# Two transformer blocks on one core: the last feed-forward's operands move to the arena and are made behind each residual

## The chip, the cores and the metric

The kernel runs on one core of a Trainium2 chip. The metric is the device time of one execution in microseconds (us). Times in the text are us from the start of the profiled span unless they are durations.

TensorE multiplies matrices, VectorE and ScalarE work elementwise, GpSimd helps with a few additions, and SyncE issues nearly all DMAs. Each engine runs its own list of instructions in order, and semaphores tie the lists together.

## What is computed

The input is one sequence of 512 tokens with 1024 features. Two blocks run one after the other. The first has a feed-forward, a mixer (a short convolution beside a gated delta rule) and another feed-forward. The second has two layers: gated linear attention with memory attention and a convolutional feed-forward, then sparse attention ("nsa") with memory attention and a convolutional feed-forward. The change touches the end of the last layer, which is in the reference:

```python
        h = h + jnp.concatenate([main.astype(xn.dtype), mo.astype(xn.dtype)], axis=-1) @ w_out[i]
        h = h + conv_ffn(rmsnorm_2(h, norm_ffn[i]), w_up[i], conv_w[i], conv_b[i], w_down[i])

def conv_ffn(x, w_up, conv_w, conv_b, w_down):
    S = x.shape[1]
    u = x @ w_up
    u_pad = jnp.pad(u, ((0, 0), (CONV_WIDTH - 1, 0), (0, 0)))
    hc = conv_b
    for j in range(CONV_WIDTH):
        hc = hc + conv_w[j] * u_pad[:, j:j + S]
    a, b = split_cols(hc, (FFN_DIM, FFN_DIM))
    return (jax.nn.silu(a) * b) @ w_down
```

FFN_DIM is 2816, so w_up has 5632 columns.

## The kernel before

The residual stream h is kept transposed in SBUF as `hT`: 128 features on the partitions, 8 blocks of features k, 512 tokens. A dense stage is a list of weight panels and output tiles. A panel of 128 output columns is 128 x 1024 fp32 values; it is loaded by SyncE into one of four slots of `raw`. Each fp32 product is made of three matmuls on two halves of either operand: the high half rounded to the type float32r, and the rest. For weights, ScalarE writes the high half wH (line 407, `split_hi`) and VectorE the low half wL = raw - wH (line 445, `split_lo`); there are two places for them, so a panel's halves can be written when TensorE has finished with the panel two before. For the activations, ScalarE writes `x_hi` = hT x gain into xH (line 826) and VectorE `x_lo` = hT x gain - xH into xL (line 831).

A tile of a features stage is 128 output features by 512 tokens in one PSUM bank. It takes 8 steps k, each of three matmuls with 512 columns: lines 570 (wH with xH), 571 (wH with xL) and 572 (wL with xH). The weights are loaded as the stationary operand and x streams past as the moving one.

The stages around the change, in order:

- The attention ends with `upper_act` (line 2763) and `rest_dve` (line 2710), which write the last pieces of xH and xL.
- `nsa_out` multiplies by w_out: 8 tiles, written as a loop of two iterations with 4 panels and banks 0 to 3. VectorE adds each finished tile to hT (line 808, called the residual below; its count is `h_from("nsa_out")`).
- `refill_act` then makes the operands of the last feed-forward on ScalarE: four squares for the norm, a wait for all matmuls of nsa_out (since they read xH), eight x_hi, the split of the next stage's panel 1 (`split_second`), four more squares. On VectorE the eight x_lo follow the last residual.
- `ffn3_up`: 11 iterations of 4 tiles, 44 tiles in all. In its first tile TensorE waits for `x_ready` step by step, so it starts when x_lo(0) is there ("GRADUAL"). GpSimd adds up the squares (line 878) and, after tile 2, TensorE sums them over the partitions (line 883); ScalarE makes `rstd` of that (lines 846, 848), and only then VectorE can evacuate tile 0 (line 2300).
- `ffn3_down`: unrolled, 22 steps over 8 banks, lines 757 to 759, with the moving operands g_hi and g_lo. Then the last norm and the output.

`gla_out`, the output stage of the layer before, has code of its own (`gla_out_pe`, lines 737 to 739): step f multiplies into all 8 banks one after the other. Its operand is m_hi, m_lo for the steps 0 and 1 and xH, xL for the steps 2 to 7.

xH, xL, wH, wL and hT are allocated one by one. The rest of SBUF is the arena: 14 regions of 2048 fp32 values per partition, of which other tensors are views at fixed offsets:

```python
        R = 2048
        at_arena = (nc.sbuf_usable_end - 4 * 14 * R) // 32 * 32
        g_hi = nc.alloc_sbuf_tensor_at("g_hi", [P, 4, S], F32R, offset=at_arena + 4 * 12 * R)
        g_lo = nc.alloc_sbuf_tensor_at("g_lo", [P, 4, S], F32R, offset=at_arena + 4 * 13 * R)
        m_hi = nc.alloc_sbuf_tensor_at("m_hi", [P, 2, S], F32R, offset=at_arena + 4 * (7 * R + R // 2))
        m_lo = nc.alloc_sbuf_tensor_at("m_lo", [P, 2, S], F32R, offset=at_arena + 4 * 7 * R)
```

In the last feed-forward, the regions 0 to 5 hold g, 6 and 8 the tiles of the convolution, 12 and 13 g_hi and g_lo. The regions 7, 9, 10 and 11 are free while ffn3_up runs.

## Time and profile before

| | us |
|---|---|
| median of 3 runs | 2510.38 (2506.29 to 2510.39) |
| the profiled execution | 2514.45 |
| its span | 2512.6 |
| TensorE busy | 2429.6 (97%) |
| VectorE busy | 1339.6 (53%) |
| ScalarE busy | 960.4 (38%) |
| GpSimd busy | 152.2 (6%) |
| nsa_out, first matmul | 2082.45 |
| ffn3_up, first matmul | 2130.22 |
| ffn3_down, first matmul | 2372.57 |

The span is the time between the first and the last record of the profiled execution; the device time around it is 1.85 us longer. TensorE's spans are modelled: each matmul is given a length that overlaps the next one's start, so the pace is read from the distance between starts, never from the lengths. A few matmul records can be missing, so a distance is taken from the first and last start and the number of steps that the program has between them.

### The profile page before, as it was taken

The page shows a single profiled execution, that of the slowest core. Times are in us where ns is not written, and L with a number is a line of the kernel's source. Part 1 is how long each engine was busy: PE and PEld are TensorE (multiplying, and loading weights), DVE is VectorE, ACT ScalarE, POOL GpSimd, SP SyncE. Part 2 cuts the span into 40 slices and gives each one's busy share as a digit, 9 for nine tenths or more (in the row PEclk, how much of TensorE's full clock was granted, in tenths as well). Part 3 has the DMA queues.
Part 4 walks back from the last instruction along what each step waited for, and adds up shares of the span by engine and source line. Part 5 has one row for each costly group of instructions (what it writes and reads, how often), then busy time and mean ns, then how long its engine had stood idle before and what let it go on. Part 6 is the DMA issues. An engine that isn't in the chain of part 4 may idle for free.

```text
span 2512.6 us, 32091 instructions
## 1 busy us (share of the span) xinstructions
PE 2429.6 (97%) x12218; PEld 1973.2 (79%) x12218; DVE 1339.6 (53%) x2054; ACT 960.4 (38%) x1461; POOL 152.2 (6%) x130
## 2 busy tenths in 40 slices
PE   7999999998999999999899999999999888999999
PEld 6888886678878888877887788878877557888887
DVE  4434337665454334345775766643535873666633
ACT  4222226632343223245334533432324773433423
POOL 3000001013010000021000100000110000000001
PEclk9999999999999999999999999999999999999999
DMA  4333222220123332223122233222843102333322
GB/s 138 92 100 93 100 85 76 76 67 10 51 76 92 100 96 88 99 85 78 47 63 76 84 98 94 92 95 90 171 140 101 45 16 67 93 100 92 101 92 76
DMA packets 319121, 215.80 MB, mean 86 GB/s; under 512 B 49289, under 2 KB 302748, under 8 KB 319016
## 3 DMA queue, kind: packets, MB, share of 16 engines
q1 hardware_dynamic: 315752, 200.40, 27.3%
q0 software_dynamic: 3264, 13.94, 1.6%
q8 instruction: 72, 1.18, 0.2%
q14 instruction: 33, 0.27, 0.0%
HBM read 212.17 MB, written 8.44 MB: 88 GB/s over the span
## 4 chain that ended last, share of the span: by engine, by line
PE 84%; DVE 8%; ACT 5%; issue 2%; DMA 1%; POOL 0%; POOLq 0%; ACTq 0%; DVEq 0%
PE bank L570 16%; PE bank L572 16%; PE bank L571 16%; PE bank L759 6%; PE bank L757 6%; PE bank L758 6%; PE bank L932 1%; DVE wL L445 1%; ACT wH L407 1%; DVE arena L2651 1%; PE bank L2138 1%; PE bank L1620 1%; PE bank L1634 1%; PE bank L2560 1%; DVE arena L2690 1%
## 5 line engine op out<-in xcount | busy, mean ns | idle before, releaser
L570 PE MATMUL bank<-xH,wH 128*128 128x512 f32 x1928 | 769.1, 399 | 14.8 <-DVE wL L445 6.4
L572 PE MATMUL bank<-xH,wL 128*128 128x512 f32 x1928 | 756.6, 392 | 0.0
L571 PE MATMUL bank<-xL,wH 128*128 128x512 f32 x1928 | 756.4, 392 | 0.0
L445 DVE TENSOR_TENSOR wL<-raw,wH 128x1024 fp32r<-128x1024 f32 (+1 forms) x357 | 448.6, 1257 | 523.6 <-ACT wH L407 522.9
L407 ACT ACTIVATE wH<-raw 128x1024 fp32r<-128x1024 f32 (+1 forms) x357 | 374.6, 1049 | 752.4 <-PE bank L572 337.5
L570 PEld LDWEIGHTS bank<-xH,wH 128*128 128x128 f32 x1928 | 363.8, 189 | 105.9 <-issue 27.1
L571 PEld LDWEIGHTS bank<-xL,wH 128*128 128x128 f32 x1928 | 363.9, 189 | 80.7 <-issue 5.3
L572 PEld LDWEIGHTS bank<-xH,wL 128*128 128x128 f32 x1928 | 363.6, 189 | 79.3 <-issue 1.2
L757 PE MATMUL bank<-g_hi,wH 128*128 128x512 f32 x704 | 277.9, 395 | 1.2 <-DVE wL L445 1.2
L759 PE MATMUL bank<-g_hi,wL 128*128 128x512 f32 x704 | 278.9, 396 | 0.0
L758 PE MATMUL bank<-g_lo,wH 128*128 128x512 f32 x704 | 278.0, 395 | 0.0
L2268 ACT ACTIVATE arena<-arena,par 128x512 f32<-128x512 f32 x88 | 63.5, 724 | 270.1 <-DVE arena L2300 270.1
L757 PEld LDWEIGHTS bank<-g_hi,wH 128*128 128x128 f32 x704 | 132.2, 188 | 34.3 <-DVE wL L445 2.5
L758 PEld LDWEIGHTS bank<-g_lo,wH 128*128 128x128 f32 x704 | 132.2, 188 | 32.5
L759 PEld LDWEIGHTS bank<-g_hi,wL 128*128 128x128 f32 x704 | 132.2, 188 | 31.7
L2300 DVE TENSOR_TENSOR arena<-bank,rstd 128x512 f32<-128x512 f32 x88 | 60.6, 691 | 86.7 <-PE bank L572 81.0
L784 ACT ACTIVATE arena<-arena 128x512 f32<-128x512 f32 x44 | 27.6, 631 | 173.8 <-DVE arena L791 173.8
L878 POOL TENSOR_TENSOR rstd<-sq 128x512 f32<-128x512 f32 x7 | 10.2, 1453 | 1289.3 <-ACT sq L841 1289.3
L793 DVE TENSOR_TENSOR arena<-bank,rstd 128x512 f32 (+1 forms) x44 | 30.2, 691 | 103.2 <-PE bank L572 103.2
L932 PEld LDWEIGHTS bank<-ident,arena 128*128 128x128 f32 (+3 forms) x402 | 46.4, 146 | 49.0 <-issue 34.4
L932 PE MATMUL bank<-ident,arena 128*128 128x128 f32 (+3 forms) x402 | 61.2, 293 | 23.2 <-DMA arena<-in_x 9.3
L791 DVE TENSOR_TENSOR arena<-bank,rstd 128x512 f32<-128x512 f32 x44 | 30.2, 691 | 85.6 <-PE bank L572 80.2
(351 smaller groups left out, 2739.2 us busy)
## 6 DMA issues: line engine op xcount, KB each, us to landing
raw<-in_ffn_w_in SPq DMA_DIRECT2D x88, 512.0 KB, 3.7
raw<-in_w_up SPq DMA_DIRECT2D x88, 512.0 KB, 3.7
raw<-in_ffn_w_out SPq DMA_DIRECT2D x44, 512.0 KB, 3.4
raw<-in_w_down SPq DMA_DIRECT2D x44, 512.0 KB, 3.5
raw<-in_w_mix_in SPq DMA_DIRECT2D x28, 512.0 KB, 3.7
raw<-in_w_kv_shared SPq DMA_DIRECT2D x12, 512.0 KB, 9.0
rel_wide<-rel_rows POOLq DMA_DIRECT2D x12, 512.0 KB, 11.0
arena<-rel_wide POOLq DMA_DIRECT2D x12, 448.0 KB, 4.1
```

The lines of the kernel that those rows point to most:

```text
L407: nc.scalar.activation(hi[:, 0:n], raw[:, k, 0:n], ACT.Copy).then_inc(sem("w_hi"), 1)
L445: nc.vector.tensor_tensor(lo[:, 0:n], raw[:, k, 0:n], hi[:, 0:n].bitcast(F32), ALU.subtract)\
L570: pe.matmul(o, wh, xa, start=a, stop=False)
L571: pe.matmul(o, wh, xb, start=False, stop=False)
L572: last = pe.matmul(o, wl, xa, start=False, stop=z)
L757: pe.matmul(bank[m][:], wh, gh, start=f == 0, stop=False)
L758: pe.matmul(bank[m][:], wh, gl, start=False, stop=False)
L759: last = pe.matmul(bank[m][:], wl, gh, start=False, stop=f == NF - 1)
L791: nc.vector.tensor_tensor(sg[:, t, :], bank[t][:], rstd[:], ALU.mult).then_inc(sem("evac_dve"), 1)
L932: return pe.transpose(o, i, ident[0:k, 0:k])
L2268: nc.scalar.activation(cv[:, t, :], us[:, t, :], ACT.Copy, scale=conv_columns(s, i, t)[2])\
L2300: nc.vector.tensor_tensor(us[:, t, :], bank[t][:], rstd[:], ALU.mult).then_inc(sem("evac_dve"), 1)
```

## The change

1. The operands of ffn3_up get tensors of their own, x2_hi (regions 9 and 10 of the arena) and x2_lo (two halves, regions 11 and 7), in place of xH and xL. `filled` and `operand` pick the tensor.
2. x_hi(k) and square(k) follow residual(k) on ScalarE within nsa_out, behind the split of the panel after the next; x_lo(k) follows residual(k+1) on VectorE. Only those of block 7 are behind the last residual. The wait for all matmuls of nsa_out is gone.
3. nsa_out has one iteration of 8 panels and 8 tiles in banks 0 to 3, 0 to 3, and is so unrolled. The same change in `out_stage` has no other user.

On ScalarE, at the end of the attention, through nsa_out (L477 is the loop) and to the norm of ffn3_up; before:

```order
L477 UNCONDITIONAL_BRANCH
L407 ACTIVATE wH<-raw 128x1024 x4
L477 REGISTER_ALU
L477 COMPARE_AND_BRANCH
L407 ACTIVATE wH<-raw 128x1024 x4
L841 ACTIVATE sq<-hT 128x512 x4
L826 ACTIVATE xH<-hT,par 128x512 x8
L407 ACTIVATE wH<-raw 128x1024
L841 ACTIVATE sq<-hT 128x512 x4
L407 ACTIVATE wH<-raw 128x1024 x3
```

and now, from the last panels of nsa_out on (line 415 is the split, 838 x_hi, 854 the square):

```order
L415 ACTIVATE wH<-raw 128x1024
L838 ACTIVATE x_hi<-hT,par 128x512
L854 ACTIVATE sq<-hT 128x512
L838 ACTIVATE x_hi<-hT,par 128x512
L415 ACTIVATE wH<-raw 128x1024
L854 ACTIVATE sq<-hT 128x512
L415 ACTIVATE wH<-raw 128x1024 x3
```

The eight x_hi and the squares, which stood together, stand now one by one behind a split each; the second x_hi in the excerpt is block 7's, ahead of the split of ffn3_up's panel 1.

On VectorE at the same place, the last two tiles of nsa_out and what follows; before:

```order
L445 TENSOR_TENSOR wL<-raw,wH 128x1024
L808 SCALAR_TENSOR_TENSOR hT<-bank,hT 128x512
L445 TENSOR_TENSOR wL<-raw,wH 128x1024
L808 SCALAR_TENSOR_TENSOR hT<-bank,hT 128x512
L831 SCALAR_TENSOR_TENSOR xL<-hT,par,xH 128x512 x8
L445 TENSOR_TENSOR wL<-raw,wH 128x1024 x4
```

and now (line 453 is the split, 816 the residual, 844 x_lo; x_lo_58 is the second half of x2_lo):

```order
L453 TENSOR_TENSOR wL<-raw,wH 128x1024
L816 SCALAR_TENSOR_TENSOR hT<-bank,hT 128x512
L844 SCALAR_TENSOR_TENSOR x_lo_58<-hT,par,x_hi 128x512
L453 TENSOR_TENSOR wL<-raw,wH 128x1024
L816 SCALAR_TENSOR_TENSOR hT<-bank,hT 128x512
L844 SCALAR_TENSOR_TENSOR x_lo_58<-hT,par,x_hi 128x512 x2
L453 TENSOR_TENSOR wL<-raw,wH 128x1024 x4
```

Six of the eight x_lo have moved ahead of the last residual.

On TensorE at the border from nsa_out (L345 ends its loop) to ffn3_up; before:

```order
L572 MATMUL bank<-xH,wL 128x512
L345 REGISTER_ALU
L345 COMPARE_AND_BRANCH
L570 MATMUL bank<-xH,wH 128x512 [waits x_ready,w_lo,evac_dve]
L571 MATMUL bank<-xL,wH 128x512
L572 MATMUL bank<-xH,wL 128x512
L570 MATMUL bank<-xH,wH 128x512 [waits x_ready]
```

and now (lines 578 to 580 are the three matmuls; x_hi is x2_hi, x_lo_57 the first half of x2_lo):

```order
L580 MATMUL bank<-xH,wL 128x512
L578 MATMUL bank<-x_hi,wH 128x512 [waits x_ready,w_lo,evac_dve]
L579 MATMUL bank<-x_lo_57,wH 128x512
L580 MATMUL bank<-x_hi,wL 128x512
L578 MATMUL bank<-x_hi,wH 128x512 [waits x_ready]
```

The loop's instructions are gone and the moving operands are the new tensors, here and in all of ffn3_up. The diff:

```diff
@@ -177,6 +177,14 @@
         m_lo = nc.alloc_sbuf_tensor_at("m_lo", [P, 2, S], F32R, offset=at_arena + 4 * 7 * R)
         m_hi_f = m_hi[:].bitcast(F32)
 
+        x2_hi = nc.alloc_sbuf_tensor_at("x2_hi", [P, KD, S], F32R, offset=at_arena + 4 * 9 * R)
+        x2_lo = [nc.alloc_sbuf_tensor_at(f"x2_lo{u}", [P, 4, S], F32R, offset=at_arena + 4 * r * R)
+                 for u, r in enumerate((11, 7))]
+
+        def operand(x, k):
+
+            return x[k // 4][:, k % 4, :] if isinstance(x, list) else x[:, k, :]
+
         def region(a, n=1):
             return arena[:, a * R:(a + n) * R]
 
@@ -203,10 +211,10 @@
             return {"bank": b, "rows": width, "cols": S, "token": False, "by": by,
                     "terms": [(j, nk, q * cols + at, width, x0 + q) for q in range(k)]}
 
-        def up_stage(k, w, f):
+        def up_stage(k, w, f, xs=(xH, xL)):
 
             return Dense(f"ffn{k}_up", NF // 2, [[panel(w, KD, c + P * u, P, 2 * P)] for c in (0, FF) for u in range(2)],
-                         [features(b, b, P, 0) for b in range(4)], (xH, xL), xfill(f))
+                         [features(b, b, P, 0) for b in range(4)], xs, xfill(f))
 
         def down_stage(k, w):
 
@@ -215,8 +223,8 @@
                       "terms": [(f, P, m * P, P, f) for f in range(NF)]} for m in range(KD)]
             return Dense(f"ffn{k}_down", 1, panels, tiles, (g_hi, g_lo), None, by_rows=True)
 
-        def ffn(k, w_in, w_out, f):
-            return [up_stage(k, w_in, f), down_stage(k, w_out)]
+        def ffn(k, w_in, w_out, f, xs=(xH, xL)):
+            return [up_stage(k, w_in, f, xs), down_stage(k, w_out)]
 
         def tokens(b, j, cols, t, by="dve"):
 
@@ -239,8 +247,8 @@
 
         def out_stage(name, w, f):
 
-            return Dense(name, 2, [[panel(w, KD, P * j, P, 4 * P)] for j in range(4)],
-                         [features(b, b, P, 0) for b in range(4)], (xH, xL), xfill(f))
+            return Dense(name, 1, [[panel(w, KD, P * j, P)] for j in range(KD)],
+                         [features(b % 4, b, P, 0) for b in range(KD)], (xH, xL), xfill(f))
 
         mem_sq = region(11).rearrange("p (k m) -> p k m", m=M)
 
@@ -325,7 +333,7 @@
                   [features((1, 0)[t % 2], t, P, 0) for t in range(6)],
                   (xH, xL), xfill(8)),
             out_stage("nsa_out", A["w_out_2"][1], 9)]
-        stages += ffn(3, A["w_up_2"][1], A["w_down_2"][1], 10)
+        stages += ffn(3, A["w_up_2"][1], A["w_down_2"][1], 10, (x2_hi, x2_lo))
         plan = Plan(stages)
         nc_block = ctx.enter_context(nc.Block())
 
@@ -560,13 +568,13 @@
                         wh, wl = hi[0:nrow, first:first + width], lo[0:nrow, first:first + width]
                         if tile["token"]:
                             o = acc[0:tile["rows"], tile["at"]:tile["at"] + width]
-                            xa, xb = xh[0:nrow, x, tile["x"]], xl[0:nrow, x, tile["x"]]
+                            xa, xb = operand(xh, x)[0:nrow, tile["x"]], operand(xl, x)[0:nrow, tile["x"]]
                             pe.matmul(o, xa, wh, start=a, stop=False)
                             pe.matmul(o, xa, wl, start=False, stop=False)
                             last = pe.matmul(o, xb, wh, start=False, stop=z)
                         else:
                             o = acc[0:width, 0:tile["cols"]]
-                            xa, xb = xh[0:nrow, x, 0:tile["cols"]], xl[0:nrow, x, 0:tile["cols"]]
+                            xa, xb = operand(xh, x)[0:nrow, 0:tile["cols"]], operand(xl, x)[0:nrow, 0:tile["cols"]]
                             pe.matmul(o, wh, xa, start=a, stop=False)
                             pe.matmul(o, wh, xb, start=False, stop=False)
                             last = pe.matmul(o, wl, xa, start=False, stop=z)
@@ -820,15 +828,20 @@
             name, at = GAINS[f]
             return column(name, at + k)
 
+        def filled(f, k):
+
+            return (x2_hi[:, k, :], operand(x2_lo, k)) if f == 10 else (xH[:, k, :], xL[:, k, :])
+
         def x_hi(act, f, k, ready):
 
             act.wait_ge(*ready)
-            nc.scalar.activation(xH[:, k, :], hT[:, k, :], ACT.Copy, scale=gain(f, k)).then_inc(sem("x_hi"), 1)
+            nc.scalar.activation(filled(f, k)[0], hT[:, k, :], ACT.Copy, scale=gain(f, k)).then_inc(sem("x_hi"), 1)
 
         def x_lo(dve, f, k):
 
+            hi, lo = filled(f, k)
             dve.wait_ge(sem("x_hi"), xbase(f) + k + 1)
-            nc.vector.scalar_tensor_tensor(out=xL[:, k, :], in0=hT[:, k, :], scalar=gain(f, k), in1=xHf[:, k, :],
+            nc.vector.scalar_tensor_tensor(out=lo, in0=hT[:, k, :], scalar=gain(f, k), in1=hi.bitcast(F32),
                                            op0=ALU.mult, op1=ALU.subtract).then_inc(sem("x_ready"), 1)
 
         def square(act, r, k, ready, scale=1.0):
@@ -3013,8 +3026,15 @@
             act.wait_ge(*matmuls_done("nsa_q"))
             mem_out_act(act, 1, xH[:, 6:8, :])
             attend_act(act)
-            dense_act(act, "nsa_out", nothing)
-            refill_act(act, 10, 7, "nsa_out", "ffn3_up")
+            residual_done = h_from("nsa_out")
+
+            def block_act(k):
+                x_hi(act, 10, k, residual_done(k))
+                square(act, 7, k, residual_done(k))
+            dense_act(act, "nsa_out", nothing, extra={(0, k + 1): lambda k=k: block_act(k) for k in range(KD - 1)})
+            x_hi(act, 10, KD - 1, residual_done(KD - 1))
+            split_second(act, "ffn3_up")
+            square(act, 7, KD - 1, residual_done(KD - 1))
             conv_up_act(act, "ffn3_up", conv_evac_act, lambda: g_first_act(act, 3), hook=lambda: rstd_act(act, 7))
             down_act(act, 3)
             last_squares_act(act)
@@ -3104,9 +3124,9 @@
             dense_dve(dve, "nsa_q", evac_scaled(aq_place, rstd[:]),
                       extra={(0, r): lambda r=r: mem_round_dve(dve, 1, r) for r in range(NROUND)})
             attend_dve(dve)
-            dense_dve(dve, "nsa_out", residual(1.0))
-            for k in range(KD):
-                x_lo(dve, 10, k)
+            dense_dve(dve, "nsa_out", residual(1.0),
+                      extra={(0, k + 1): lambda k=k: x_lo(dve, 10, k) for k in range(KD - 1)})
+            x_lo(dve, 10, KD - 1)
             conv_up_dve(dve, "ffn3_up", conv_evac_dve, lambda: g_first_dve(dve, 3), hook=lambda: norm_dve(dve, 7))
             conv_end_dve(dve, "ffn3_up")
             down_dve(dve, 3, 1.0, None)
```

## Rows read from the trace of the kernel before

**Rows 1.** The page's head: span; engine, busy time, share, instructions.

```profile
span 2512.6 us, 32091 instructions
PE 2429.6 (97%) x12218; PEld 1973.2 (79%) x12218; DVE 1339.6 (53%) x2054; ACT 960.4 (38%) x1461; POOL 152.2 (6%) x130
```

**Rows 2.** Timeline of TensorE, nsa_out's end: start, duration, instruction, [idle before, releaser].

```profile
2127.50 0.39 PE L572 MATMUL bank<-xH,wL 128*128 128x512 f32 x1
2130.22 0.47 PE L570 MATMUL bank<-xH,wH 128*128 128x512 f32 x1 [2.33 <-DVE xL L831]
2130.53 0.44 PE L571 MATMUL bank<-xL,wH 128*128 128x512 f32 x1
...
2131.19 0.63 PE L570 MATMUL bank<-xH,wH 128*128 128x512 f32 x1
...
2134.17 0.39 PE L571 MATMUL bank<-xL,wH 128*128 128x512 f32 x1
```

**Rows 3.** Stretches: length, engines' busy time (instructions), TensorE's granted clock, DMA share, GB/s.

```profile
2130.90:2134.10 3.20, 3.20 (x9) 2.51 (x8) 3.20 (x6) 3.20 (x6) 0.00 (x0) 0.50 0.00 0
...
2160.00:2360.00 200.00, 199.90 (x882) 165.21 (x881) 136.88 (x171) 76.47 (x98) 0.00 (x0) 1.00 0.32 96
```

**Rows 4.** Timeline of ScalarE, nsa_out's end and ffn3_up's start.

```profile
2122.55 1.06 ACT L407 ACTIVATE wH<-raw 128x1024 fp32r<-128x1024 f32 x1 [4.38 <-PE bank L572]
...
2127.93 5.01 ACT L826 ACTIVATE xH<-hT,par 128x512 fp32r<-128x512 f32 x8 [0.66 <-PE bank L572]
```

**Rows 5.** Timeline of VectorE, the same stretch.

```profile
2127.93 0.69 DVE L808 SCALAR_TENSOR_TENSOR hT<-bank,hT 128x512 f32<-128x512 f32 x1 [3.06 <-PE bank L572]
2128.68 6.03 DVE L831 SCALAR_TENSOR_TENSOR xL<-hT,par,xH 128x512 fp32r<-128x512 f32 x8
2134.63 1.21 DVE L445 TENSOR_TENSOR wL<-raw,wH 128x1024 fp32r<-128x1024 f32 x1
2140.13 2.24 DVE L445 TENSOR_TENSOR wL<-raw,wH 128x1024 fp32r<-128x1024 f32 x1 [4.29 <-ACT wH L407]
```

**Rows 6.** Instructions by line, 2085 to 2136: ns min/median/max, first and last start.

```profile
L831 DVE SCALAR_TENSOR_TENSOR xL<-hT,par,xH x8: 737/737/1389, 2128.7 to 2134.0; 128x512 fp32r<-128x512 f32 x8
L826 ACT ACTIVATE xH<-hT,par x8: 706/706/722, 2127.9 to 2132.2; 128x512 fp32r<-128x512 f32 x8
L841 ACT ACTIVATE sq<-hT x4: 613/616/633, 2123.5 to 2126.7; 128x512 f32<-128x512 f32 x4
```

**Rows 7.** Timeline of GpSimd, all of it from 2060 to 2190.

```profile
2124.74 1.28 POOL L878 TENSOR_TENSOR rstd<-sq 128x512 f32<-128x512 f32 x1 [101.65 <-ACT sq L841]
2126.82 2.70 POOL L878 TENSOR_TENSOR rstd<-rstd,sq 128x512 f32<-128x512 f32 x2 [0.81 <-ACT sq L841]
2134.49 6.80 POOL L878 TENSOR_TENSOR rstd<-rstd,sq 128x512 f32<-128x512 f32 x4 [4.96 <-ACT sq L841]
```

**Rows 8.** One matmul line of gla_out (L738), of ffn3_down (L758), of nsa_out (L571).

```profile
L738 PE MATMUL bank<-xL,wH x48: 388/389/398, 1354.2 to 1386.2; 128*128 128x512 f32 x48
...
L738 PE MATMUL bank<-m_lo,wH x16: 394/394/394, 1343.0 to 1353.5; 128*128 128x512 f32 x16
...
L758 PE MATMUL bank<-g_lo,wH x167: 398/399/400, 2380.0 to 2496.2; 128*128 128x512 f32 x167
...
L571 PE MATMUL bank<-xL,wH x60: 389/389/395, 2087.1 to 2127.3; 128*128 128x512 f32 x60
```

**Rows 9.** Timelines of VectorE and TensorE, the attention's end and nsa_out's start.

```profile
2080.71 1.41 DVE L2710 TENSOR_TENSOR xL<-bank,xH 64x512 fp32r<-64x512 f32 x2 [7.01 <-ACT xH L2763]
...
2082.45 0.49 PE L570 MATMUL bank<-xH,wH 128*128 128x512 f32 x1 [2.42 <-DVE xL L2710]
```

**Rows 10.** Timelines of TensorE and VectorE, the norm and first evacuation of ffn3_up.

```profile
2148.23 1.03 PE L883 MATMUL bank<-rstd,ones 128*128 128x512 f32 x2
...
2153.53 1.29 DVE L2300 TENSOR_TENSOR arena<-bank,rstd 128x512 f32<-128x512 f32 x2 [2.72 <-ACT rstd L848]
...
2154.57 0.39 PE L570 MATMUL bank<-xH,wH 128*128 128x512 f32 x1
```

## The prediction

> **What bounds the kernel now.** I read the engines' busy shares first: TensorE is busy 97% of 2512.6 us [rows 1], so a change counts if it moves TensorE's idle time or the pace of its matmuls, and nothing else does. Next I read TensorE's instructions in order of time where nsa_out ends and ffn3_up begins, and looked for a break in the spacing of starts. The last matmul of nsa_out starts at 2127.50, the first of ffn3_up at 2130.22, after 2.33 us of idle that ends with VectorE's L831 [rows 2]. From 2131.19 to the eleventh matmul at 2134.17, starts are 2.98 / 7 = 0.43 us apart, against 0.227 elsewhere [rows 2, 8], and in that stretch the granted clock is 0.50, so 1.2 GHz in place of the 2.4 GHz of the steady part of ffn3_up, which shows 1.00 [rows 3]. The engine had idled for 2.33 us just before.
>
> Why it idles: ScalarE may write xH only when nsa_out's last matmul has read it, so x_hi starts at 2127.93 and needs 0.706 us for one [rows 4, 6]. VectorE's first x_lo starts at 2128.68 and takes 1389 ns in place of the usual 737, while GpSimd has two adds running from 2126.82 for 2.70 us [rows 6, 7]; 2128.68 + 1.39 = 2130.07, and the matmul starts 0.15 later.
>
> The third view is the one that this change turns on: one line's instructions, sorted by the tile that they read, with count and first and last start. In gla_out, the same three lines of code run with moving operands m_hi, m_lo for 16 steps of three matmuls and xH, xL for 48 steps. With m_lo: (1353.5 - 1343.0) / 15 = 0.700 us a step; with xL: (1386.2 - 1354.2) / 47 = 0.681 [rows 8]. ffn3_down, whose moving operands are g_hi and g_lo, gives (2496.2 - 2380.0) / 166 = 0.700; nsa_out, with xH and xL, (2127.3 - 2087.1) / 59 = 0.681 [rows 8]. So a matmul starts every 0.2333 us or every 0.2267. The weights lie in wH and wL in all four. gla_out changes its bank after every step with either operand, so the bank does not set the pace. What the slow ones share is that m_hi, m_lo, g_hi and g_lo lie in the arena, and xH, xL don't.
>
> **The change part by part.**
> The pause goes. In nsa_out each residual(k) is now followed by x_hi(k), and x_lo(k) by residual(k+1). With nsa_out's end where it is in the trace: x_lo(0) to x_lo(5) are done before it; residual(7) still runs 2127.93 to 2128.62; x_lo(6) follows, 0.74, to 2129.4; x_hi(7) starts at about 2128.7, ends 2129.4; x_lo(7) ends at 2130.2 [rows 5, 6]. TensorE goes on at 2127.73, takes six k-steps with what is ready, and asks for x_lo(6) at 2127.73 + 6 x 0.70 = 2131.9 and x_lo(7) at 2132.6: 2.5 and 2.4 us to spare. Even the stretched 1.39 of an x_lo [rows 6] is covered. What this saves: the eleventh matmul would have started at 2127.50 + 11 x 0.2267 = 2129.99 and started at 2134.17: **-4.18 us**, 2.5 of it idle and 1.7 clock.
>
> What is late next: panel 1's halves, for tile 1 at 2127.73 + 24 x 0.2333 = 2133.33. On ScalarE its wH now stands behind x_hi(7): 2129.4 to 2130.4, a split taking 1.06 [rows 4]; VectorE's wL then 1.21, to 2131.7, or 2.24 if GpSimd adds beside it, as at 2140.13 [rows 5], to 2132.7. The margin is 0.6 to 1.6 us. Cost nil; if the cover goes, TensorE idles here instead.
>
> Work put into nsa_out. Per tile ScalarE gets 0.71 + 0.62 us more, VectorE 0.74 and GpSimd an add of about 1.3 [rows 6, 7]; the tiles are 8 x 0.681 = 5.45 us apart. On VectorE, counted from the start of tile k+1 (2127.73 for the last), residual(k) runs from +0.2 to +0.9, x_lo(k-1) to +1.6 and wL for panel k+2 to +2.9, or +3.9 if stretched; it is wanted at +5.45. ScalarE's wH for that panel comes ahead of x_hi(k), so it doesn't move. GpSimd has waited there since the attention, so the adds start at once. Cost nil, 1.5 us of cover.
>
> The norm for ffn3_up: squares and adds now end near 2132.5 rather than 2141.3, but the sum matmul L883 stands behind tile 2 as before, and the first evacuation starts 5.3 us after it (2148.23, 2153.53), 1.0 us before tile 4 wants its bank (2154.57) [rows 10]. All of these hang on TensorE's own place and move with it: nil.
>
> The unrolling. Before, TensorE waits in front of the loop and then enters it; its first matmul of nsa_out comes 0.33 us after the last L2710 ends (2080.71 + 1.41 = 2082.12, then 2082.45) [rows 9], against 0.15 at ffn3_up, which has no loop there. Now the wait stands on the matmul. That bounds it between -0.18 and 0; I take **-0.18**, since ffn3_up's first step is the same code. Inside nsa_out the loop costs nothing to remove: its steps are at 0.681 across both iterations. More instructions to fetch: ffn3_down is unrolled and steady, so nil.
>
> **The new home.** All 44 tiles of ffn3_up, 8 k-steps each, now read x2_hi and x2_lo as the moving operand: 352 steps. x2_hi is in regions 9 and 10 of the arena, x2_lo in 11 and 7; region 7 begins with the very addresses of m_lo. The price is bounded by 0 (if what slows m and g weren't their place) and 352 x (0.700 - 0.680) = +7.04. Three tensors at three places in the arena show it, one of them at an address that x2_lo takes over, and nothing else separates the two rows of L738 [rows 8]; I take **+7.04**. Nothing hides it, as TensorE is the bound and has no idle time inside ffn3_up.
> The Trainium skill, in "TensorE: Matmul & The Clock Gate", section "Wait — 56ns, not 53.3ns?", gives bf16 matmuls in a row a spacing of N / 2.4 GHz + 2.5 ns, so 215.7 ns at 512 columns, with no word on where the operand lies. Rows 8 have 227 and 233 ns for this fp32 form. By that rule the home is free and the sum is the two savings alone; by the rows it is not.
>
> Sum: 7.04 - 4.18 - 0.18 = **+2.7 us**. The profiled execution took 2514.45 (its span 2512.6), so one like it would take 2517.1. The median of the runs shown is 2510.38, so I predict 2513.1, or +0.11%.
>
> **The rivals.**
> (a) The home is free. Then the step is 0.681 throughout ffn3_up and only the savings are left: 2510.38 - 4.36 = 2506.0. For it: the rows show two rates, not their cause, and x2_hi's regions 9 and 10 are read by no such matmul in the trace. Against: gla_out's own contrast, and region 7. In the Trainium skill, "SBUF — State Buffer", section "SBUF: two separate sides", says that only VectorE and GpSimd contend for a port and that TensorE waits for nobody; by it this rival would be the forecast.
> (b) Slower: the pause comes back one tile later. If wL of panel 1 comes after 2133.33, TensorE stops in front of tile 1. It decides at a delay of 1.6 us against my timing, 0.6 if GpSimd's last add stretches that wL. ScalarE's order x_hi(7), wH, square(7) puts the add right beside it, which speaks for it; that the two rows of stretching are at most 1.0 us speaks against. A stop of some 2 us with the clock at 0.50 behind it gives the 4.18 back, leaving 7.04 - 0.18 = +6.9: 2517.3, slower by 0.27%. The same price if wL runs late inside nsa_out.
> (c) The change doesn't do what it says: TensorE still stops at the start of ffn3_up, for x_lo(6) or x_lo(7), because ScalarE's chain runs more than 2.4 us late. The price is as in (b) or less. It needs GpSimd to hold up square(k), and with it the x_hi behind it; an add has 5.45 us per tile and took at most 2.7 for two.
> (d) The home costs more than in the rows, if here ScalarE and VectorE write beside it in the arena. Before, they also wrote there during ffn3_down. I can't bound it from a row above 0.700.
>
> **How the numbers follow.** Forecast 0.76, (a) 0.12, (b) 0.07, (c) and (d) 0.05 together. About 0.2% of this kernel, 5 us, is what a measurement can tell from no change: below 2505.4 is faster, above 2515.4 slower. The runs shown lie 4 us apart, so of the forecast's share some 0.05 falls above 2515.4; (b), (c), (d) fall there but for 0.02; (a) is 0.6 us from the lower edge and gives 0.04 to faster. That makes faster 0.04, slower 0.15, same 0.81. The range is from 2506.0, which is (a)'s value, to 2517.0, the forecast's value with the spread of the runs, short of (b).
>
> **What would show it.** In the trace of the changed kernel: no idle of TensorE before ffn3_up's first matmul and a granted clock of 1.00 from 2086 to the end of ffn3_down (pause); starts 0.700 us a step through ffn3_up, (last - first) / (count - 1) for the line of x_lo (home), where 0.681 would prove (a); no TensorE idle released by L445's successor at tile 1 (else (b)); nsa_out's first matmul about 0.15 after the last x_lo of the attention (unrolling). From nsa_out's first matmul to ffn3_down's first, 2.9 us more than before (7.04 - 4.18). I'm wrong if ffn3_up runs at 0.681, or if a wait shows between 2127 and 2140 that I have not named.

## The result

| | before | changed |
|---|---|---|
| median, us (22 executions each) | 2506.23 | 2514.12 |
| lowest to highest | 2504.97 to 2511.98 | 2508.54 to 2518.40 |
| ratio, 95% interval | | 1.0022 (1.0015 to 1.0028) |
| the profiled execution, and its span | 2514.45, 2512.6 | 2514.33, 2512.6 |

The change makes the kernel 5.5 us slower by the ratio; I forecast 2.7 us slower, and a time of 2513.1. The times of either kernel come in two groups 5 to 6 us apart, and the ratio mixes two things: how far the groups have moved and how many executions fall in each. Over all executions of this study, the kernel before has 38 of 74 in its lower group (mean 2506.1) and 36 in its upper (2511.3); the changed kernel has 10 of 34 in its lower (2509.3) and 24 in its upper (2515.4). Group against group the change costs 3.3 and 4.1 us. The two profiled executions are no fair pair by their spans: the profiled one of the kernel before, 2514.45, is slower than all 22 in the table. In the changed kernel's trace nsa_out also begins 2.15 us earlier (2080.30 against 2082.45), and only 0.3 of that is due to the change.

The page's head of the changed kernel answers to [rows 1]:

```profile
span 2512.6 us, 32066 instructions
PE 2433.7 (97%) x12218; PEld 1973.3 (79%) x12218; DVE 1337.6 (53%) x2054; ACT 959.9 (38%) x1461; POOL 151.5 (6%) x130
```

TensorE at the border of nsa_out and ffn3_up, where [rows 2] have 2.33 us of idle (start, duration, instruction):

```profile
2123.74 0.39 PE L580 MATMUL bank<-xH,wL 128*128 128x512 f32 x1
2123.96 0.40 PE L578 MATMUL bank<-x_hi,wH 128*128 128x512 f32 x1
2124.20 0.40 PE L579 MATMUL bank<-x_lo,wH 128*128 128x512 f32 x1
2124.43 0.40 PE L580 MATMUL bank<-x_hi,wL 128*128 128x512 f32 x1
```

The starts stand 0.22 to 0.24 us apart across the border: no idle. Two stretches of the changed kernel (length, TensorE's busy time and matmuls, granted clock, DMA share and GB/s): the first lies in the output part and shows 1.2 GHz, the second is ffn3_up and shows no slow clock:

```profile
2499.20:2502.60 3.40, 3.40 (x18) 0.50 0.00 0
2124.00:2370.00 246.00, 246.00 (x1054) 1.00 0.31 93
```

ScalarE and VectorE after the last matmul of nsa_out, against [rows 4, 5]:

```profile
2124.89 0.72 ACT L838 ACTIVATE x_hi<-hT,par 128x512 fp32r<-128x512 f32 x1 [3.91 <-DVE hT L816]
2125.52 1.04 ACT L415 ACTIVATE wH<-raw 128x1024 fp32r<-128x1024 f32 x1
2126.47 0.62 ACT L854 ACTIVATE sq<-hT 128x512 f32<-128x512 f32 x1
...
2124.16 0.69 DVE L816 SCALAR_TENSOR_TENSOR hT<-bank,hT 128x512 f32<-128x512 f32 x1 [2.95 <-PE bank L580]
2124.77 1.63 DVE L844 SCALAR_TENSOR_TENSOR x_lo<-hT,par,x_hi 128x512 fp32r<-128x512 f32 x2
2126.59 1.23 DVE L453 TENSOR_TENSOR wL<-raw,wH 128x1024 fp32r<-128x1024 f32 x1 [0.19 <-ACT wH L415]
```

Both x_lo are done at 2124.77 + 1.63 = 2126.4, 2.4 us after ffn3_up began; they are wanted after 4.2 and 4.9. wL of panel 1 is done at 2127.8 and wanted at 2129.6, and GpSimd's last add (2127.16, 1.81 us) did not stretch it. So rivals (b) and (c) are out.

At nsa_out's start, against [rows 9] (VectorE, then TensorE):

```profile
2078.84 1.41 DVE L2723 TENSOR_TENSOR xL<-bank,xH 64x512 fp32r<-64x512 f32 x2 [7.01 <-ACT xH L2776]
...
2080.30 0.50 PE L578 MATMUL bank<-xH,wH 128*128 128x512 f32 x1 [2.13 <-DVE xL L2723]
```

The first matmul comes 0.05 us after x_lo's end at 2080.25, in place of 0.33.

From nsa_out's first matmul to ffn3_down's first I had expected 2.9 us more than before. It is 0.8 more: 290.93 us against 290.12, the 2372.57 - 2082.45 of the kernel before. The changed kernel's end of that stretch:

```profile
2371.23 0.39 PE L765 MATMUL bank<-g_hi,wH 128*128 128x512 f32 x1
```

The kernel before began nsa_out at 1.2 GHz, the changed one didn't (first before, then changed):

```profile
2082.90:2086.20 3.30, 3.30 (x10) 0.51 0.45 132
```

```profile
2080.30:2087.00 6.70, 6.70 (x29) 1.00 0.27 81
```

That is not the change's doing: experiments 6 and 11, which have the change's order of work, begin nsa_out at 1.2 GHz too, and experiments 3 and 10, which haven't, don't. The stretch must be compared between traces that agree in this.

### The profile page after: what moved, and what is told of

Its sections match the earlier page's. It is cut to its first block, busy times and chain, and to the rows that moved or that the text cites. A ratio compares the mean times of both kernels' runs of the same rounds, so it can differ in the third digit from the quotient of the medians.

```text
span 2512.6 us, 32066 instructions
## 1 busy us (share of the span) xinstructions
PE 2433.7 (97%) x12218; PEld 1973.3 (79%) x12218; DVE 1337.6 (53%) x2054; ACT 959.9 (38%) x1461; POOL 151.5 (6%) x130
## 4 chain that ended last, share of the span: by engine, by line
PE 86%; DVE 7%; ACT 5%; issue 1%; DMA 0%; POOL 0%; POOLq 0%; ACTq 0%; DVEq 0%
PE bank L578 17%; PE bank L579 16%; PE bank L580 16%; PE bank L767 6%; PE bank L766 6%; PE bank L765 6%; PE bank L945 1%; DVE arena L2664 1%; DVE wL L453 1%; PE bank L2151 1%; PE bank L1633 1%; PE bank L2573 1%; PE bank L1647 1%; ACT wH L415 1%; PE bank L1642 1%
## 5 line engine op out<-in xcount | busy, mean ns | idle before, releaser
L578 PE MATMUL bank<-xH,wH 128*128 128x512 f32 (+1 forms) x1576 | 629.4, 399 | 12.1 <-DVE wL L453 6.5
L580 PE MATMUL bank<-xH,wL 128*128 128x512 f32 (+1 forms) x1576 | 617.4, 392 | 0.0
L579 PE MATMUL bank<-xL,wH 128*128 128x512 f32 (+1 forms) x1576 | 617.4, 392 | 0.0
L578 PEld LDWEIGHTS bank<-xH,wH 128*128 128x128 f32 (+1 forms) x1576 | 296.9, 188 | 87.8 <-issue 21.3
L579 PEld LDWEIGHTS bank<-xL,wH 128*128 128x128 f32 (+1 forms) x1576 | 296.8, 188 | 66.0 <-issue 4.6
L580 PEld LDWEIGHTS bank<-xH,wL 128*128 128x128 f32 (+1 forms) x1576 | 296.6, 188 | 65.2 <-issue 0.7
L579 PE MATMUL bank<-x_lo,wH 128*128 128x512 f32 x352 | 140.3, 399 | 0.0
L578 PE MATMUL bank<-x_hi,wH 128*128 128x512 f32 x352 | 139.1, 395 | 0.0
L580 PE MATMUL bank<-x_hi,wL 128*128 128x512 f32 x352 | 138.1, 392 | 0.0
L2313 DVE TENSOR_TENSOR arena<-bank,rstd 128x512 f32<-128x512 f32 x88 | 60.6, 691 | 92.8 <-PE bank L580 87.2
```

What stands on the lines that cost most here:

```text
L578: pe.matmul(o, wh, xa, start=a, stop=False)
L579: pe.matmul(o, wh, xb, start=False, stop=False)
L580: last = pe.matmul(o, wl, xa, start=False, stop=z)
L2313: nc.vector.tensor_tensor(us[:, t, :], bank[t][:], rstd[:], ALU.mult).then_inc(sem("evac_dve"), 1)
```

## The experiments

**1. The new home alone.** The order of work is taken back, the home is kept:

```diff
-            return Dense(name, 1, [[panel(w, KD, P * j, P)] for j in range(KD)],
-                         [features(b % 4, b, P, 0) for b in range(KD)], (xH, xL), xfill(f))
+            return Dense(name, 2, [[panel(w, KD, P * j, P, 4 * P)] for j in range(4)],
+                         [features(b, b, P, 0) for b in range(4)], (xH, xL), xfill(f))
...
-            dense_act(act, "nsa_out", nothing, extra={(0, k + 1): lambda k=k: block_act(k) for k in range(KD - 1)})
...
+            dense_act(act, "nsa_out", nothing)
+            refill_act(act, 10, 7, "nsa_out", "ffn3_up")
...
-            dense_dve(dve, "nsa_out", residual(1.0),
-                      extra={(0, k + 1): lambda k=k: x_lo(dve, 10, k) for k in range(KD - 1)})
-            x_lo(dve, 10, KD - 1)
+            dense_dve(dve, "nsa_out", residual(1.0))
+            for k in range(KD):
+                x_lo(dve, 10, k)
```

> The kernel of the change with its order of work taken back: nsa_out is again a loop of two iterations and x_hi, the squares and x_lo follow the last residual as before, but into the new tensors in the arena. My theory (the home costs 20 ns on each of 352 steps, the pause is worth 4.2 us): the pause and the stretch at 1.2 GHz stay, ffn3_up runs at 0.700 us a step, and the time is 7.0 us above the kernel before (ratio 1.0028). Rival (the home is free and something in the new order costs the time): ratio 1.000, steps at 0.681.

Ratio 1.0021 (1.0011 to 1.0030), 11 executions. Its groups are 5 at 2511.8 to 2512.8 and 6 from 2517.4 up, so group against group it costs 6 to 7 us; the ratio is lower since in the same session the kernel before had 16 of 23 executions in its upper group. The pause is there, and the matmuls that read x_lo (first the pause, then the line's count and first and last start from 2136.5 on):

```profile
2129.43 0.48 PE L578 MATMUL bank<-x_hi,wH 128*128 128x512 f32 x1 [2.33 <-DVE x_lo L844]
...
L579 PE MATMUL bank<-x_lo,wH x345: 394/394/399, 2136.2 to 2377.9; 128*128 128x512 f32 x173
```

The same line of the kernel before, which starts at the same place by chance:

```profile
L571 PE MATMUL bank<-xL,wH x345: 387/389/395, 2136.2 to 2371.4; 128*128 128x512 f32 x173
```

Over the same 345 matmuls, 241.7 us against 235.2: the home costs 6.5 us. That it isn't 344 x 0.020 = 6.9 has its row in the kernel before. Its tile 5 begins at 2160.01 and should end 5.44 later at 2165.45:

```profile
2165.23 0.39 PE L572 MATMUL bank<-xH,wL 128*128 128x512 f32 x1
2165.72 0.50 PE L570 MATMUL bank<-xH,wH 128*128 128x512 f32 x1
```

Tile 6 begins at 2165.72, 0.27 late, and it takes 0.13 too long itself (2165.72 to 2171.29 is 5.57). In the traces of experiment 1 and of the changed kernel the tiles 5 and 6 take exactly 5.60 each, at 0.700 a step: a wait of 0.40 us, which the view doesn't list as idle, now lies under the slower matmuls.

**2. The unrolling alone.**

```diff
-            return Dense(name, 2, [[panel(w, KD, P * j, P, 4 * P)] for j in range(4)],
-                         [features(b, b, P, 0) for b in range(4)], (xH, xL), xfill(f))
+            return Dense(name, 1, [[panel(w, KD, P * j, P)] for j in range(KD)],
+                         [features(b % 4, b, P, 0) for b in range(KD)], (xH, xL), xfill(f))
```

> The kernel before with nsa_out alone unrolled (one iteration of 8 panels). My theory: TensorE's first matmul of nsa_out comes about 0.05 us after the attention's last x_lo instead of 0.33, so -0.3 us, ratio 0.9999, which can't be told from 1. Rival (the longer instruction list costs time, here or earlier, and explains why the change came out 2 to 3 us above my sum): +3 us, ratio 1.001.

Ratio 1.0002 (0.9991 to 1.0013), 12 executions. VectorE, then TensorE:

```profile
2078.62 1.41 DVE L2710 TENSOR_TENSOR xL<-bank,xH 64x512 fp32r<-64x512 f32 x2 [7.01 <-ACT xH L2763]
...
2080.09 0.50 PE L570 MATMUL bank<-xH,wH 128*128 128x512 f32 x1 [2.13 <-DVE xL L2710]
```

0.06 us again. The unrolling is worth 0.3 us by the trace and nothing that a time can show. The interval alone would still allow the rival's 3 us; the groups don't: the 4 executions of the lower one have a mean of 2505.9 against 2505.8 for the kernel before in the same session, the 8 of the upper one 2512.2 against 2511.3.

**3 and 4. The arena 32 bytes lower.** In the kernel before and in the changed one:

```diff
-        at_arena = (nc.sbuf_usable_end - 4 * 14 * R) // 32 * 32
+        at_arena = (nc.sbuf_usable_end - 4 * 14 * R) // 64 * 64
```

> The kernel before with the arena's start rounded down to a multiple of 64 bytes instead of 32, which moves it by 32 bytes and changes nothing else. Theory A (the moving operand's start address sets the pace: 32 bytes past a multiple of 64 costs 6.7 ns a matmul): ffn0 to ffn3_down (4 x 176 steps) and gla_out's first 16 steps go from 0.700 to 0.680 a step, 720 x 0.020 = -14.4 us, ratio 0.9943. Theory B (the place in the arena costs, whatever the address): the steps stay at 0.700 and the ratio is 1.000.

> The kernel of the change with the same rounding to 64 bytes. Theory A: ffn3_up too runs at 0.680, the pause stays gone, so before - 14.4 - 4.5 = about -18.9 us, ratio 0.9925, and 4.5 us faster than the kernel before with the same rounding. Theory B: as the change itself, ratio 1.002, steps at 0.700.

Ratios 0.9955 (0.9942 to 0.9968) and 0.9953 (0.9940 to 0.9966). Moving the arena by 32 bytes takes 11 us off the kernel before. Theory B is out; theory A had the cause and not the whole size. Experiment 4 was to be 4.5 us below experiment 3 and is 0.8 below by the means: ffn3_up at 0.687 a step instead of 0.680 takes back 352 x 0.0067 = 2.4 us, and a longer output part, treated below, 1.1 to 1.6. gla_out's line, with m_lo and with xL, in the kernel before with this rounding:

```profile
L738 PE MATMUL bank<-xL,wH x48: 389/389/398, 1347.2 to 1379.2; 128*128 128x512 f32 x48
...
L738 PE MATMUL bank<-m_lo,wH x16: 388/392/392, 1336.2 to 1346.5; 128*128 128x512 f32 x16
```

With m_lo (1346.5 - 1336.2) / 15 = 0.687 a step, where [rows 8] have 0.700, and xL stays at 0.681. The arena now lies 64 bytes past a multiple of 128, while xH, xL, wH and wL lie on one (by the order and sizes in which they are allocated; no trace shows an address), which gave the next step.

**5 and 6. The arena on a multiple of 128.**

```diff
-        at_arena = (nc.sbuf_usable_end - 4 * 14 * R) // 32 * 32
+        at_arena = (nc.sbuf_usable_end - 4 * 14 * R) // 128 * 128
```

> The kernel before with the arena's start rounded down to a multiple of 128 bytes (it lies 96 bytes past one in the kernel before; with the rounding to 64 it lay 64 past one, and ffn3_down ran at 0.687 to 0.691 a step, half way). xH, xL, wH and wL lie at multiples of 128. Theory A' (the moving operand's start modulo 128 sets the pace): all dense steps at 0.680, ffn3_down in 119.7 us in place of 123.9, so 720 x 0.020 = -14.4 us on the kernel before, ratio 0.9943, 3 to 4 us below the 64-byte version. Rival (64 is all that counts, and the 0.687 comes from something else): as the 64-byte version, ratio 0.9955.

> The kernel of the change with the same rounding to 128 bytes. Theory A': ffn3_up at 0.680 a step, so the home is free and the early operands show their own worth: 4.2 us for the pause, of which up to 1.7 may be lost again in the output part when the slow clock there lasts 6.8 us instead of 3.4, as in the changed kernel. So 2.5 to 4.5 us below the 128-byte version of the kernel before, ratio about 0.993 to the kernel before. Rival (0.687 stays): 1 us below it or less.

Ratios 0.9943 (0.9931 to 0.9956) and 0.9946 (0.9933 to 0.9959). The kernel before with this rounding, ffn3_down and gla_out:

```profile
L758 PE MATMUL bank<-g_lo,wH x163: 389/389/389, 2370.0 to 2480.2; 128*128 128x512 f32 x163
...
L738 PE MATMUL bank<-m_lo,wH x16: 389/389/395, 1335.3 to 1345.5; 128*128 128x512 f32 x16
```

(1345.5 - 1335.3) / 15 = 0.680. All of the 14.4 us that 720 steps were to give is there: 0.9943 is 14.3 us. In the changed kernel, ffn3_up's 351 steps take 240.0 us where they take 246.6 without the rounding; the home is free at this address (changed kernel with the rounding first, then without):

```profile
L579 PE MATMUL bank<-x_lo,wH x352: 387/389/395, 2113.7 to 2353.7; 128*128 128x512 f32 x176
```

```profile
L579 PE MATMUL bank<-x_lo,wH x352: 394/399/402, 2124.2 to 2370.8; 128*128 128x512 f32 x176
```

The two executions profiled here both begin nsa_out at 1.2 GHz, so they show the worth of the pause without a price of the home beside it. The starts of nsa_out's and of ffn3_down's first matmul, in experiment 5 and then in 6:

```profile
2069.74 0.70 PE L570 MATMUL bank<-xH,wH 128*128 128x512 f32 x1 [2.42 <-DVE xL L2710]
...
2359.84 0.39 PE L757 MATMUL bank<-g_hi,wH 128*128 128x512 f32 x1
```

```profile
2068.15 0.50 PE L578 MATMUL bank<-xH,wH 128*128 128x512 f32 x1 [2.13 <-DVE xL L2723]
...
2354.11 0.39 PE L765 MATMUL bank<-g_hi,wH 128*128 128x512 f32 x1
```

290.10 us against 285.96: the pause is worth 4.1 us. The times showed none of the 2.5 to 4.5 us that I had expected of experiment 6: both have a mean of 2495.0. Experiment 5 has 3 of 6 executions in a lower group (2492.3) and 3 in an upper (2497.8), experiment 6 has all 5 between 2494.1 and 2496.6.

Not every form of matmul pays for its address. These plain fp32 matmuls of 256 columns stream a moving operand out of the arena, in the kernel before and in experiment 5:

```profile
1113.37 7.07 PE L554 MATMUL bank<-arena,raw 128*128 128x256 f32 x32
```

```profile
1106.89 7.07 PE L554 MATMUL bank<-arena,raw 128*128 128x256 f32 x32
```

32 of them take 7.07 us at either address, so what is said here of the address holds for the float32r form with 512 columns.

**7. xH and xL moved to the arena's residue.** They lie 96 bytes past a multiple of 128 in this one, as the arena does in the kernel before:

```diff
+        sb("pad0", [P, 24])
         xH = sb("xH", [P, KD, S], F32R)
         xL = sb("xL", [P, KD, S], F32R)
+        sb("pad1", [P, 8])
```

> The kernel before with 96 unused bytes allocated ahead of xH and 32 behind xL, so that xH and xL lie 96 bytes past a multiple of 128, as the arena's tensors do, and all else keeps its place modulo 128. Theory A (address): every stage on xH and xL goes from 0.680 to 0.700 a step; about 2072 steps x 0.020 = +41 us, ratio 1.016. Theory B (the arena as a place): 0.680 stays, ratio 1.000.

One execution, 2539.17 against 2506.9, the median before: 32 us slower, ratio 1.013 with no interval. nsa_out's line 573, the former 571:

```profile
L573 PE MATMUL bank<-xL,wH x60: 392/396/463, 2104.3 to 2145.7; 128*128 128x512 f32 x60
```

41.4 us for the 59 steps that take 40.2 in [rows 8], 0.70 each: tensors outside the arena slow down just so. Why not 41? Experiment 8, below, is an execution of the same group with an arena just as slow. Compared with it matmul by matmul, its 6032 spacings of 0.20 to 0.26 us on xH and xL, outside the stretches at 1.2 GHz, grow by 37.2 us; the others shrink by 4.8, and those stretches add 0.6. The sum of 33.0 is the difference of the two spans (2537.4 against 2504.0) but for 0.4. So some 5 us of the price were made up in the other spacings, the longer ones above all, in which TensorE waits.

**8. The arena at the fourth residue,** `// 128 * 128 + 32`.

> The kernel before with the arena's start 32 bytes past a multiple of 128 instead of 96. One look for the step of ffn3_down at the fourth residue: 0.680 at 0, 0.687 at 64 and 0.700 at 96 are measured or expected. If the price grows with the distance to the next lower multiple of 128, about 0.683; if being off a multiple of 64 is what costs, 0.700 again. Time between 14 us below the kernel before and equal to it accordingly.

One execution, 2505.8, in the lower group of the kernel before; ffn3_down:

```profile
L758 PE MATMUL bank<-g_lo,wH x168: 390/394/397, 2370.8 to 2487.7; 128*128 128x512 f32 x168
```

(2487.7 - 2370.8) / 167 = 0.700. So the step is 0.680 at a multiple of 128, 0.687 at 64 past one, and 0.700 at 32 and at 96.

**9, 10 and 11. What the early operands are worth alone, and the groups.** The changed kernel once more; the new home alone with the arena on a multiple of 128; the changed kernel with it, in the same session.

> The changed kernel once more, for its distribution. The times of one kernel come in two groups some 5 us apart (22 executions of the kernel before: 15 near 2505.8 and 7 near 2511; 22 of the changed one: 7 near 2509.2 and 15 near 2514.5), and the traces of the other runs show the difference between groups ahead of nsa_out. My theory: which group an execution falls in has nothing to do with the change, so the shares come out about even for both here, and each group of the changed kernel lies 3 to 4 us above that of the kernel before: ratio 1.0014. Rival: the change itself moves executions to the upper group; then 2 in 3 are up again and the ratio is 1.002 or more.

> The new home alone, order of work as before, with the arena at a multiple of 128. My theory (the home's price is its address): equal to the 128-byte version of the kernel before, ratio to the kernel before 0.9943 (within 0.1%), ffn3_up at 0.680 a step. Rival (another price of the home): up to 6.6 us more, 0.997.

> The changed kernel with the arena at a multiple of 128 once more, beside the run above in the same chip session: their difference is the early operands and the unrolling alone. The trace has 4.2 us less up to ffn3_down and 1.6 us more in the output part, where the slow clock lasted 6.8 us rather than 3.4. If the longer output part comes with the early order every time, 2.5 us below the run above; if it is chance, 4.2 on average of the two; if the two cancel, 0.

Ratios 1.0022 (1.0011 to 1.0033), 0.9944 (0.9928 to 0.9960) and 0.9931 (0.9913 to 0.9948). The home at a good address costs nothing: experiment 10 has the ratio of experiment 5. For the early operands: the 6 executions with the old order are 2492.4, 2493.0 and 2496.1 to 2498.2, the 6 with the early order 2487.4, 2488.0 and 2493.8 to 2496.0. The two lower groups are 5.0 us apart, the upper ones 1.9. By the means of all 6, experiment 11 is 2.9 us below. The 11 executions of 6 and 11 have a mean of 2493.7, the 12 of 5 and 10 one of 2495.3; group against group the early order is worth 2.3 us in the upper one (9 against 7 executions) and 4.7 in the lower (2 against 5). The trace says where much of the 4.2 us goes in the upper group. TensorE's sums and transposes behind ffn3_down, first in the old order (experiment 10), then in the early one (experiment 11):

```profile
2479.54 1.84 PE L2811 MATMUL bank<-ones,arena 128*128 128x1 f32 x16
2481.24 1.07 PE L945 MATMUL bank<-ident,hT 128*128 128x128 f32 x8
2482.15 2.74 PE L2811 MATMUL bank<-ones,arena 128*128 128x1 f32 x24
```

```profile
2476.39 1.84 PE L2811 MATMUL bank<-ones,arena 128*128 128x1 f32 x16
2478.09 1.07 PE L945 MATMUL bank<-ident,hT 128*128 128x128 f32 x8
2478.99 4.67 PE L2811 MATMUL bank<-ones,arena 128*128 128x1 f32 x24
```

The same 24 small matmuls take 4.67 us in place of 2.74. In the kernels with the arena on a multiple of 128 the granted clock behind ffn3_down is this (experiment 5, then 6):

```profile
2483.00:2486.00 3.00, 3.00 (x30) 1.00 0.00 0
2486.60:2489.60 3.00, 3.00 (x16) 0.50 0.00 0
```

```profile
2478.90:2484.90 6.00, 6.00 (x29) 0.50 0.00 0
```

The clock falls to 1.2 GHz behind ffn3_down in every kernel. From ffn3_down's last matmul to TensorE's last instruction it is 11.3 us in all five traces with the early order, and 9.4 to 9.7 in seven of the nine with the old one (the others are experiments 1 and 12, 11.3 and 11.1). Up to the end of the span, which has about 6 us more behind TensorE's last instruction, the difference is 1.3 us between the two profiles of before and changed, 1.1 between experiments 3 and 4, 1.8 between 5 and 6, 1.9 between 10 and 11. The cost is shown, 1.1 to 1.9 us; what makes the early order fall on the long side is not, and experiments 1 and 12 show that the old order can fall there too.

On the groups: experiment 9 has 3 of 12 in the lower group where the kernel before had 10 of 17, so my expectation of even shares was not met. Of the traces, those of experiments 7 and 8 have the mean clock of lower-group executions (0.987). Experiment 8 and the changed kernel in the mixer, from 420 to 510 us:

```profile
420.00:510.00 90.00, 86.34 (x340) 62.91 (x339) 56.91 (x84) 55.91 (x76) 0.00 (x0) 0.98 0.28 74
```

```profile
420.00:510.00 90.00, 86.33 (x327) 62.41 (x326) 56.10 (x83) 56.90 (x77) 0.00 (x0) 0.94 0.26 70
```

A clock of 0.98 against 0.94, and 13 matmuls more in the same time. Up to 2045 us, ahead of the changed code, the stretches at 1.2 GHz add up to 47.8 us in each of experiments 7 and 8 and to 54.6 to 64.9 in the other twelve traces: the difference between the groups, or most of it, arises before nsa_out. By that the change should not move the shares. 10 of 34 against 38 of 74 speaks mildly for the contrary, and is left open.

**12. The stationary operand.** The 128-byte version of the kernel before with wH and wL moved:

```diff
+        sb("pad0", [P, 24])
         wH = sb("wH", [P, 2, SLOT], F32R)
         wL = sb("wL", [P, 2, SLOT], F32R)
+        sb("pad1", [P, 8])
```

> The 128-byte version of the kernel before with wH and wL, the stationary operands, moved 96 bytes past a multiple of 128 (24 unused values ahead of wH, 8 behind wL); the moving operands keep their place. If only the moving operand's address counts: dense steps stay at 0.680, time as the 128-byte version, about 2495. If the stationary operand's counts as well: 0.700 for all steps of ffn up and down too, some 2800 steps x 0.020 = +56 us, about 2550.

One execution, 2547.63: 53 us above experiment 5's median of 2494.65, and 50 or 55 above its two groups. nsa_out's line:

```profile
L573 PE MATMUL bank<-xL,wH x48: 392/397/400, 2113.7 to 2146.7; 128*128 128x512 f32 x48
```

(2146.7 - 2113.7) / 47 = 0.702 a step, with both moving operands on a multiple of 128. The address of the weights counts as much as that of the operand that streams past. Whether each address counts for itself, or the difference of the two modulo 128, these runs can't tell: in all of them the pace is best where both lie on a multiple of 128, and one of the two always did.

## Why the prediction was right, and where not

The direction and the two large terms held, and the measured 2514.12 lies in the range and 1.0 us from 2513.1. That it lies so near is partly luck. The sum came out too small: 2.7 us against 3.3 and 4.1 by groups, and 5.5 by the ratio, just outside the 0.2% that I had given 0.81 to. But the 2510.38 that I added it to was the median of three executions, two of them from the upper group, and 4.2 us above the 2506.23 of all 22. From 2506.23 the same sum gives 2508.9, still in the range and 5.2 below the measured time.

- **The home, +7.04: 0.5 us too large.** Measured 6.5 by experiment 1 (from nsa_out's first matmul to ffn3_down's first, 296.65 us against 290.12). The step "nothing hides it, as TensorE has no idle time inside ffn3_up" failed: 0.40 us of waiting in tiles 5 and 6 was there, too short for the list of idle times, and visible only as a tile of 5.71 instead of 5.44. The bet that the new home costs was made on a contrast within one stage [rows 8], and it held. What I named as the common trait of the slow operands was that they lie in the arena; experiments 3, 5 and 7 show that it is their address, not the arena.
- **The pause, -4.18: right,** 4.1 by experiments 5 and 6. From nsa_out's first matmul to ffn3_down's first, the changed kernel takes 2.4 us more than experiment 2 (290.93 against 288.52), whose nsa_out also starts at full clock and which has the pause; my terms without the loop say 2.86, and the hidden 0.40 is most of the difference. The 2.9 that I announced against the kernel before itself came out as 0.8, since that one began nsa_out at 1.2 GHz, which costs 1.6 us (290.12 against 288.52).
- **The unrolling, -0.18:** 0.28 by two traces, outside the bounds of 0 and 0.18 that I had set. The 0.15 us at ffn3_up's first matmul were no floor for nsa_out's, which comes after 0.05.
- **"All of these hang on TensorE's own place and move with it: nil"** was right for the norm, and I carried it silently on to the end of the kernel. There it failed: the output part took 11.28 us instead of the 9.56 of the kernel before, because the granted clock was low for 6.8 us from 2499.1 and not for 3.4 from 2502.8. It gives back 1.7 of the 4.2 us, or 1.3 counted to the end of the span. The cause of that is open, since two traces of the old order have it too. With the home at 6.64 (7.04 less the 0.40) the sum is 6.64 - 4.18 - 0.28 + 1.7 = 3.9, or 3.5 with 1.3, which is near the upper group's 4.1; of the changed kernel's lower group no trace exists.
- **The measurement.** I took the spread of the runs for noise of 4 us. It is two groups, with 5 to 6 us between them, and the ratio depends on how many executions fall in which. That can be the rest between 3.3 to 4.1 and 5.5.
- **Rivals.** (a) fell with experiments 1, 3 and 5: 227 or 233 ns depend on an address. The Trainium skill, "TensorE: Matmul & The Clock Gate", section "Wait — 56ns, not 53.3ns?", gives 215.7 ns at 512 columns with no word on the address; the float32r matmuls here take 227 ns at best, so the measurement decides. (b) and (c) fell with the trace. (d) fell with it too: ffn3_up in the changed kernel keeps the 0.700 a step of [rows 8].

With the arena on a multiple of 128 bytes the changed kernel beats both: means of 2493.7 against 2495.3 for the same arena in the old order, and against 2506.1 and 2511.3 for the groups of the kernel before. Nearly all of that gain is the address; the 1.6 us of the early operands is no more than these few executions can carry, though both groups point the same way.

## What to carry to other kernels

Before a tensor gets a new home, compare the spacing of starts of the instructions that read it with those that read its neighbours there; one line of code with two kinds of operand is the best such pair. Place what TensorE reads in this form, moving or stationary, on a multiple of 128 bytes, and check the start of any hand-made arena. Time taken out ahead of a stretch that runs at a changing clock may come back in part behind it, so measure to the last instruction and not to the end of the stage.

## What the runs showed of the hardware

| start of the moving operand modulo 128 bytes | step of three fp32r matmuls, 512 columns | per matmul |
|---|---|---|
| 0 | 0.680 us | 227 ns |
| 64 | 0.687 us | 229 ns |
| 32 or 96 | 0.700 us | 233 ns |
| 0, with the stationary one at 96 | 0.702 us | 234 ns |

The 229 and 233 ns were the same in every stage that reads the arena; those of 32 and of the last row come from one execution each. Both operands off a multiple of 128 was not tried. I had not expected the address to matter for the weights, which are loaded beside the running matmul (0.188 us of 0.227). The Trainium skill, "SBUF — State Buffer", section "Operand start alignment", gives the multiple that a start address must keep and says that this is about legality, not speed; these runs add the speed.
